# Second FFN of a two-block transformer layer: the modulation's place in the first steps, and its row products on TensorE

## The chip, the cores and the metric

One core of a Trainium2 chip runs the whole program. TensorE (PE) multiplies matrices into PSUM banks, VectorE (DVE), ScalarE (ACT) and GpSimd (POOL) work beside it, and SyncE (SP) and POOL issue the transfers that this text speaks of. The metric is the device time of one execution, in microseconds (us), as the median of several runs.

## The reference

Two transformer blocks follow each other on 512 tokens of width 1024. The first ends with a SwiGLU feed-forward network (here the second FFN of the program, called ffn2). The second block scales and shifts its norms by a modulation vector made from a conditioning vector c alone:

```python
x = x + 0.5 * swiglu(rms_norm(x, ffn2_norm[l]), ffn2_w_gate[l], ffn2_w_up[l], ffn2_w_down[l])
def swiglu(h, w_gate, w_up, w_down):
    return (jax.nn.silu(h @ w_gate) * (h @ w_up)) @ w_down
...
mod = (c_act @ w_mod[l] + b_mod[l])[:, None, :]      # c_act = silu(c), w_mod 1024 x 6144
sh1, sc1, g1, sh2, sc2, g2 = jnp.split(mod, N_MOD, axis=-1)
```

The second block also has an S5 state-space part, whose tables (powers and rotations of the state matrix, kernels inside chunks) depend on parameters alone.

## The kernel before

A weight matrix is read in panels of 1 MB (128 partitions x 2048 values). SP loads a panel into w_raw, ACT rounds it to its high part w_hi (L692), DVE subtracts to get the low part w_lo (L1188, split), and PE makes three products for each pair of tiles: high by high, low by high and high by low. There are two buffers of each kind: the gate panels use one, the up panels the other. SP loads the next panel into a buffer as soon as w_split says that its low part is made.

The gate and up products of ffn2 run over 11 steps. In a step PE makes 48 matmuls of the gate panel into banks 0 and 1 (by_k, L2004), then 48 of the up panel into banks 2 and 3. DVE scales the gate banks by the norm's root (L1391, "gate scaling"), ACT takes the SiLU, DVE multiplies by the up banks (L1401), and splits the product into high and low parts for the down product (L1236).

The first eight steps of ffn2 carry other work beside this, each in a loop of its own (PHASES). Steps 0 to 3 carry the last four of the modulation's twelve groups (ffn1's steps carry the first eight). For a group, DVE multiplies eight tiles of w_mod by one value of c_act per partition and adds them up (modulation, L1352 and L1355), splits the sum in two (L1360, L1362), and PE sums it over the partitions by two matmuls with a one-hot matrix (L2044, the row products), which put the group in a row of bank 6. POOL loads the tiles of w_mod, 256 KB each, into four slots (L568): the first four tiles of a group are there when it begins, and the load of tile 4 waits for DVE's use of tile 0, and so on, so that half of a group's tiles are loaded while it is computed. DVE may begin a group only when PE has made the row products of the group before it (semaphore mod_acc_free), since low part and sum lie in one place.

Behind each of the steps 0 to 3, DVE computes a part of the S5 tables (setup: s5_matrices, s5_first_angles, s5_second_angles, s5_powers). Steps 4 to 7 carry two pairs of chunk matrices each: DVE makes one pair ahead of the gate scaling and one behind the gate panel's low part (prepared, L1318 to L1329, 12 instructions each), and PE takes them behind the up products (chunk_pair, L2071 and L2080), first pair 0 and then pair 1. From step 4 on, prepared's first pair also waits until all twelve groups are in bank 6. All this is program order on each engine: an instruction that waits holds up whatever stands behind it.

Of the kernel before, what the change touches and what calls it, by code (L numbers as in the profile page):

```python
# [64 lines left out]
MOD_SLOTS = 4  # L65

MOD_STEPS = KD + 2
# [9 lines left out]
MOD_END = MOD_GROUPS - BESIDE_STEPS  # L77
# [3 lines left out]
MOD_STOP = {"ffn1": BESIDE_STEPS, "ffn2": MOD_END}  # L81
MOD_AT = {"ffn1": 0, "ffn2": BESIDE_STEPS}
# [50 lines left out]
def build(nc, inp, rel_onehot, out):  # L133
# [12 lines left out]
    with ExitStack() as ctx:  # L146
# [5 lines left out]
        def S(name):  # L152
            if name not in sems:
                sems[name] = ctx.enter_context(nc.semaphore(name))
            return sems[name]

        B = [ctx.enter_context(nc.psum_tensor(f"bank{i}", [P, T], F32)) for i in range(8)]
# [23 lines left out]
        row_of = sb("row_of", [P, 8], F32R)  # L181
# [183 lines left out]
        def paired(extra):  # L365

            return extra is not None and extra >= MOD_END
# [806 lines left out]
        def _(dve):  # L1174
            done = Steps(dve, S("dve_done"))

            def split(n, i=None):

                if i is None:
                    if n >= END:  # L1180
                        return
                    i = n
                dve.wait_ge(S("w_hi_done"), n + 1)
                if not isinstance(n, int) or n:

                    dve.wait_ge(S("w_split"), n)
                s = i % 2
                dve.tensor_tensor(w_lo[s][:], w_raw[s][:], w_hi[s][:].bitcast(F32), ALU.subtract).then_inc(S("w_split"), 1)  # L1188
# [175 lines left out]
            def swiglu(name):  # L1364
                base = BASE[name]
                setup = (s5_matrices, s5_first_angles, s5_second_angles, s5_powers)
                for start, stop, mods, extra in PHASES[name]:
                    if start == BESIDE_STEPS:

                        groups = sum(b - a for f in list(PHASES)[:list(PHASES).index(name) + 1] for a, b, m, _ in PHASES[f] if m)  # L1370
                        dve.wait_ge(S("mod_acc_free"), groups + 1)
                        dve.tensor_copy(tmp[0:8, 4, :], B[6][0:8, :]).then_inc(S("rows_made"), 1)
                        if name == "ffn2":
                            dve.wait_ge(S("pair_pe"), NS // 2)
                            for r in range(2):
                                dve.wait_ge(S(f"ca_stored{r}"), 32 * 4)
                                dve.wait_ge(S(f"pair_stored{r}"), 128 * 4)
                    with dve.Fori(start, stop) as i:
                        if start == 0:
                            modulation(i + MOD_AT[name], i, range(MOD_SLOTS))  # L1380
                            refined_root({"ffn1": "n1", "ffn2": "n2"}[name])
                            if name == "ffn1":
                                modulation(i + MOD_AT[name], i, range(MOD_SLOTS, KD))
                        elif mods:
                            modulation(i + MOD_AT[name], i)
                        if paired(extra):
                            prepared(extra, 0)
                        for t in range(2):
                            dve.wait_ge(S("pe_done"), i * 8 + (4 * base + 2 * t + 2))
                            dve.wait_ge(S("hid"), i * 2 + (HID[name] + t + 1))  # L1390
                            dve.tensor_tensor(tmp[:, t, :], B[t][:], rstd[:], ALU.mult).then_inc(S("gate_scaled"), 1)  # L1391
                        if start == 0 and name == "ffn2":
                            modulation(i + MOD_AT[name], i, range(MOD_SLOTS, KD))
                        split(i * 2 + (base + 2), base)
                        if paired(extra):
                            prepared(extra, 1)
                        for t in range(2):
                            dve.wait_ge(S("pe_done"), i * 8 + (4 * base + 4 + 2 * t + 2))
                            dve.wait_ge(S("silu"), i * 2 + (HID[name] + t + 3))
                            dve.wait_ge(S("hid_split"), i * 2 + (HID[name] + t + 1))  # L1400
                            dve.tensor_tensor(tmp[:, 2 + t, :], tmp[:, t, :], B[2 + t][:], ALU.mult).then_inc(S("hid"), 1)  # L1401
                        split(i * 2 + (base + 3), base + 1)
                        for t in range(2):
                            hid_lo_of(name, i, t, 2 + t)
                        if paired(extra):
                            kernels_read(extra)
                    if extra in range(MOD_END):
                        setup[extra]()

                first = 4 * MOD_AT[name]  # L1410
                last_col = 4 * groups
                dve.wait_ge(S("rows_t"), 2 * list(PHASES).index(name) + 5)
                turned = B[5][:, 0:32].rearrange("p (s g) -> p g s", s=4)[:, 0:groups - MOD_AT[name], :]
                dve.tensor_tensor(mod[:, first:last_col].rearrange("p (g s) -> p g s", s=4), turned,
                                  cols("b_mod_2")[:, first:last_col].rearrange("p (g s) -> p g s", s=4), ALU.add).then_inc(S("mod_made"), 1)
# [509 lines left out]
        def _(pe):  # L1925
# [83 lines left out]
            def first_gate(n, banks, h_name, between):  # L2009
# [10 lines left out]
                for k in range(KD):  # L2020
                    for t, bank in enumerate(banks):
                        mm = pe.matmul(bank[:], wl[:, k, t * P:(t + 1) * P], h_hi[:, k, :], start=False, stop=k == KD - 1)
                        if k == KD - 1:
                            mm.then_inc(S("pe_done"), 2)

            def gate_up(name, h_name, free, sums=None):

                base = BASE[name]
                for start, stop, mods, extra in PHASES.get(name, ((0, GU_STEPS, False, None),)):
                    with pe.Fori(start, stop) as i:  # L2030
                        for half in range(2):
                            if sums and start == 0 and half == 0:
                                first_gate(base, [B[0], B[1]], h_name, sums)
                                continue
                            pe.wait_ge(S("w_split"), i * 2 + (base + half + 1))
                            free(i, half)
                            wait = not sums and half == 0
                            by_k(base + half, [B[2 * half], B[2 * half + 1]], h_hi, h_lo, ready(h_name) if wait else None,
                                 wait_hi=ready_hi(h_name) if wait else None)
                        if mods:  # L2040

                            pe.wait_ge(S("mod_step"), i * MOD_STEPS + ((MOD_AT[name] + 1) * MOD_STEPS + MOD_SLOTS))
                            for part in (mod_hi, mod_lo):
                                mm = pe.matmul(B[6][0:8, :], row_of[:], part[:],  # L2044
                                               start=start == 0 and part is mod_hi, stop=stop == MOD_STOP[name] and part is mod_lo)
                            mm.then_inc(S("mod_acc_free"), 1)
                        if paired(extra):
                            for r in range(2):
                                chunk_pair(extra, r)
                    if name in PHASES and stop == GU_STEPS:  # L2050
                        pe.wait_ge(S("rows_made"), 2 * list(PHASES).index(name) + 2)
                        for s4 in range(4):
                            mm = pe.transpose(B[5][:, 8 * s4:8 * s4 + 8], tmp[0:8, 4, s4 * P:(s4 + 1) * P], ident[0:8, 0:8])
                        mm.then_inc(S("rows_t"), 1)
                    if name == "ffn2" and extra == 0:

                        pe.wait_ge(S("s5_landed"), 320)
                        for part in range(2):
                            for c in range(4):
                                mm = pe.transpose(B[4 + part][:, c * P:(c + 1) * P], c_in[:, part, c].rearrange("p w n -> p (w n)"), ident[:])  # L2060
                            mm.then_inc(S("c_t"), 1)
# [55 lines left out]
            for k in range(KD):  # L2117
# [3 lines left out]
                for b in range(TB):  # L2121
                    mm = pe.transpose(B[2 + k % 4][:, b * P:(b + 1) * P], x_in[:, b, k * P:(k + 1) * P], ident[:])
# [98 lines left out]
            for f in range(2):  # L2221
                for g in range(4):
                    mm = pe.transpose(B[6 + f][:, g * P:(g + 1) * P], ws_in[:, 4 * f + g, :], ident[:])
# [8 lines left out]
            for f in range(4):  # L2232
                for c in range(TB):
                    for half in range(2):
                        g = 2 * f + half
                        mm = pe.matmul(B[4 + f][64 * half:64 * half + 64, c * P:(c + 1) * P],
                                       vg[:, c, g * 64:(g + 1) * 64], wsT[:, g, :], start=True, stop=True)
# [406 lines left out]
```

## Time and profile before

| what | value |
|---|---|
| median of 3 runs | 1794.73 us (1794.62 to 1794.98) |
| profiled execution | 1793.39 us, span from first to last instruction 1791.9 us |
| PE busy | 1763.9 us, 98% of the span |
| DVE busy | 1069.7 us, 60% |
| ACT busy | 729.3 us, 41% |
| mean granted clock of PE | 0.999 of full speed |
| steps 1 to 4 of ffn2 | about 861 to 956 us from the span's start |

Lines in the views are those of the kernel before. The idle time in brackets stands ahead of an instruction on its engine, with what ended it. A busy PE is a pipeline with work in it, so stalls show as gaps between its rows.

### The profile page before, as it was taken

To read this page: it belongs to the slowest core of one execution; us is meant where nothing else is said; L and a number is where in the kernel's file an instruction comes from. 1 tells how busy PE (TensorE), PEld (TensorE's weight loads), DVE (VectorE), ACT (ScalarE), POOL (GpSimd) and SP (SyncE) were. 2 spreads that over 40 slices of the span, in tenths; PEclk is the share of its full clock that TensorE was granted. 3 is DMA by queue.
4 is the path that set the end of the run, shared out by engine and by line. 5 is a ranking of instruction groups with operands and counts; after the bars stand their busy time and mean duration, and the time that the engine had idled before them with its cause. 6 is when DMAs were issued, how large, how long until landed. Compare 5 with 4: busy or idle time off the path is not lost. (4 is left out here: it accounts for less than half of the span.)

```text
span 1791.9 us, 23429 instructions
## 1 busy us (share of the span) xinstructions
PE 1763.9 (98%) x8822; PEld 1437.1 (80%) x8822; DVE 1069.7 (60%) x1507; ACT 729.3 (41%) x1001; POOL 186.1 (10%) x239
## 2 busy tenths in 40 slices
PE   9999999999999999999999999999999999999998
PEld 6888888888887777788877888887986788888887
DVE  7666546655655676656888743436595655566433
ACT  4222222333435877423333222225465355555322
POOL 4222001210000000005211110210000300000000
PEclk9999999999999999999999999999999999999999
DMA  7777423343222121224554552325122222222232
GB/s 246 238 221 221 134 74 96 98 138 99 90 95 94 48 66 53 71 94 150 173 188 125 158 158 66 107 93 187 68 79 68 93 95 94 94 94 82 94 95 81
DMA packets 171694, 206.81 MB, mean 115 GB/s; under 512 B 18404, under 2 KB 150114, under 8 KB 171106
## 3 DMA queue, kind: packets, MB, share of 16 engines
q1 hardware_dynamic: 144994, 161.97, 27.9%
q0 software_dynamic: 12640, 38.55, 6.7%
q10 hardware_dynamic: 13984, 5.27, 1.1%
q8 instruction: 49, 0.80, 0.2%
q14 instruction: 27, 0.22, 0.0%
HBM read 190.29 MB, written 17.56 MB: 116 GB/s over the span
## 5 line engine op out<-in xcount | busy, mean ns | idle before, releaser
L692 ACT CAST w_hi<-w_raw 128x2048 fp32r<-128x2048 f32 x158 | 301.8, 1911 | 722.4 <-PE bank L2004 360.9
L1188 DVE TENSOR_TENSOR w_lo<-w_raw,w_hi 128x2048 fp32r<-128x2048 f32 x158 | 367.3, 2325 | 358.4 <-ACT w_hi L692 357.7
L2004 PE MATMUL bank<-h_hi,w_hi 128*128 128x512 f32 x1056 | 412.3, 390 | 3.5 <-DVE w_lo L1188 2.2
L2004 PE MATMUL bank<-h_hi,w_lo 128*128 128x512 f32 x1056 | 411.1, 389 | 0.0
L2004 PE MATMUL bank<-h_lo,w_hi 128*128 128x512 f32 x1056 | 325.4, 389 | 1.6 <-DVE h_lo L1231 1.6
L2004 PEld LDWEIGHTS bank<-h_hi,w_hi 128*128 128x128 f32 x1056 | 198.2, 188 | 49.5 <-issue 3.4
L2004 PEld LDWEIGHTS bank<-h_lo,w_hi 128*128 128x128 f32 x1056 | 198.2, 188 | 43.3 <-DVE h_lo L1231 2.0
L2004 PEld LDWEIGHTS bank<-h_hi,w_lo 128*128 128x128 f32 x1056 | 198.3, 188 | 41.0
L1961 PE MATMUL bank<-hid_hi,w_hi 128*128 128x512 f32 x528 | 205.6, 389 | 0.0
L1961 PE MATMUL bank<-hid_hi,w_lo 128*128 128x512 f32 x528 | 205.4, 389 | 0.0
L1961 PE MATMUL bank<-hid_lo,w_hi 128*128 128x512 f32 x528 | 205.4, 389 | 0.0
L611 POOL TENSOR_TENSOR tmp<-x 128x512 f32<-128x512 f32 x24 | 37.2, 1549 | 867.1 <-DVE x L1762 422.7
L1961 PEld LDWEIGHTS bank<-hid_hi,w_lo 128*128 128x128 f32 x528 | 99.1, 188 | 20.7
L1961 PEld LDWEIGHTS bank<-hid_hi,w_hi 128*128 128x128 f32 x528 | 99.1, 188 | 20.6
L1961 PEld LDWEIGHTS bank<-hid_lo,w_hi 128*128 128x128 f32 x528 | 99.1, 188 | 20.4
L1961 PE MATMUL bank<-w_hi,h_hi 128*128 128x512 f32 (+1 forms) x256 | 97.4, 380 | 0.7 <-DVE h_lo L1231 0.7
L1961 PE MATMUL bank<-w_hi,h_lo 128*128 128x512 f32 (+1 forms) x256 | 96.3, 376 | 0.0
L1961 PE MATMUL bank<-w_lo,h_hi 128*128 128x512 f32 (+1 forms) x256 | 96.2, 376 | 0.0
L1355 DVE SCALAR_TENSOR_TENSOR mod_acc<-mod_raw,small,mod_acc 128x512 f32<-128x512 f32 x84 | 63.1, 752 | 29.7 <-DMA mod_raw<-in_w_mod 25.6
L568 POOL DMA_DIRECT2D mod_raw<-in_w_mod x96 | 52.7, 550 | 174.5 <-DVE mod_acc L1352 123.1
L1401 DVE TENSOR_TENSOR tmp<-tmp,bank 128x512 f32<-128x512 f32 x44 | 28.3, 684 | 67.1 <-PE bank L2004 67.1
L1909 DVE SCALAR_TENSOR_TENSOR tmp<-bank,vec,tmp 128x511 f32<-128x511 f32 x88 | 63.8, 746 | 6.4 <-DVE tmp L1909 1.7
(442 smaller groups left out, 2464.8 us busy)
## 6 DMA issues: line engine op xcount, KB each, us to landing
w_raw<-in_w_in SPq DMA_DIRECT2D x29, 1024.0 KB, 5.0
mod_raw<-in_w_mod POOLq DMA_DIRECT2D x96, 256.0 KB, 4.1
w_raw<-in_ffn_w_gate SPq DMA_DIRECT2D x22, 1024.0 KB, 5.2
w_raw<-in_ffn_w_up SPq DMA_DIRECT2D x22, 1024.0 KB, 5.2
w_raw<-in_w_up SPq DMA_DIRECT2D x22, 1024.0 KB, 4.9
w_raw<-in_ffn_w_down SPq DMA_DIRECT2D x16, 768.0 KB, 4.6
w_raw<-in_ffn_w_down SPq DMA_DIRECT2D x16, 640.0 KB, 4.0
w_raw<-in_w_out SPq DMA_DIRECT2D x8, 1024.0 KB, 5.0
```

The source lines that it names most:

```text
L568: pool.dma_start(mod_raw[:, k % MOD_SLOTS, :], wm[:, k, bass.ds(i * T + first * T, T)])\
L611: done(pool.tensor_tensor(tmp[:, min(k, 1), :], x[:, k, :], x[:, k, :], ALU.mult))
L692: act.copy(w_hi[i % 2][:], w_raw[i % 2][:]).then_inc(S("w_hi_done"), 1)
L1188: dve.tensor_tensor(w_lo[s][:], w_raw[s][:], w_hi[s][:].bitcast(F32), ALU.subtract).then_inc(S("w_split"), 1)
L1355: ins = dve.scalar_tensor_tensor(mod_acc[:], mod_raw[:, k % MOD_SLOTS, :], small[:, k:k + 1], mod_acc[:], ALU.mult, ALU.add)
L1401: dve.tensor_tensor(tmp[:, 2 + t, :], tmp[:, t, :], B[2 + t][:], ALU.mult).then_inc(S("hid"), 1)
L1909: dve.scalar_tensor_tensor(y[:, back:], up[:, :T - back], col_at(f"conv_w_2:{2 - back}", i * 2, KF * half + t), y[:, back:], ALU.mult, ALU ...
L1961: mm = pe.matmul(out_ap, stationary, moving, start=first and i == 0, stop=last and i == total - 1)
L2004: mm = pe.matmul(bank[:], w[:, k, at], h[:, k, :], start=k == first and part == 0 and i == 0, stop=k == last and part == 1)
```

## The change

In the steps 1 to 3 of ffn2, DVE computes the modulation's group behind the gate scaling and the gate panel's low part, instead of ahead of both. On PE the row products of a group stand no longer behind the up products of its step: they stand between the gate and the up products of the next step (so group 0 of ffn2 in step 1, and group 3 in step 4, where no group is computed). ffn1 and ffn2's step 0 on DVE stay as they were.

```diff
--- before.py
+++ after.py
@@ -1381,7 +1381,7 @@
                             refined_root({"ffn1": "n1", "ffn2": "n2"}[name])
                             if name == "ffn1":
                                 modulation(i + MOD_AT[name], i, range(MOD_SLOTS, KD))
-                        elif mods:
+                        elif mods and name == "ffn1":
                             modulation(i + MOD_AT[name], i)
                         if paired(extra):
                             prepared(extra, 0)
@@ -1392,6 +1392,8 @@
                         if start == 0 and name == "ffn2":
                             modulation(i + MOD_AT[name], i, range(MOD_SLOTS, KD))
                         split(i * 2 + (base + 2), base)
+                        if mods and start and name == "ffn2":
+                            modulation(i + MOD_AT[name], i)
                         if paired(extra):
                             prepared(extra, 1)
                         for t in range(2):
@@ -2023,6 +2025,13 @@
                         if k == KD - 1:
                             mm.then_inc(S("pe_done"), 2)
 
+            def mod_rows(name, i, first, last, behind=0):
+
+                pe.wait_ge(S("mod_step"), i * MOD_STEPS + ((MOD_AT[name] + 1 - behind) * MOD_STEPS + MOD_SLOTS))
+                for part in (mod_hi, mod_lo):
+                    mm = pe.matmul(B[6][0:8, :], row_of[:], part[:], start=first and part is mod_hi, stop=last and part is mod_lo)
+                mm.then_inc(S("mod_acc_free"), 1)
+
             def gate_up(name, h_name, free, sums=None):
 
                 base = BASE[name]
@@ -2037,13 +2046,10 @@
                             wait = not sums and half == 0
                             by_k(base + half, [B[2 * half], B[2 * half + 1]], h_hi, h_lo, ready(h_name) if wait else None,
                                  wait_hi=ready_hi(h_name) if wait else None)
-                        if mods:
-
-                            pe.wait_ge(S("mod_step"), i * MOD_STEPS + ((MOD_AT[name] + 1) * MOD_STEPS + MOD_SLOTS))
-                            for part in (mod_hi, mod_lo):
-                                mm = pe.matmul(B[6][0:8, :], row_of[:], part[:],
-                                               start=start == 0 and part is mod_hi, stop=stop == MOD_STOP[name] and part is mod_lo)
-                            mm.then_inc(S("mod_acc_free"), 1)
+                            if name == "ffn2" and half == 0 and start in range(1, MOD_END + 1):
+                                mod_rows(name, i, start == 1, start == MOD_END, 1)
+                        if mods and name == "ffn1":
+                            mod_rows(name, i, start == 0, stop == MOD_STOP[name])
                         if paired(extra):
                             for r in range(2):
                                 chunk_pair(extra, r)
```

DVE, step 1 of ffn2, in program order: ahead of it are the last rows of s5_matrices, behind it s5_first_angles. Before:

```order
L1378 UNCONDITIONAL_BRANCH
L1348 CAST row_of<-one_hot 128x8
L1352 TENSOR_SCALAR mod_acc<-mod_raw,small 128x512
L1355 SCALAR_TENSOR_TENSOR mod_acc<-mod_raw,small,mod_acc 128x512 x7
L1360 CAST mod_hi<-mod_acc 128x512
L1362 TENSOR_TENSOR mod_lo<-mod_acc,mod_hi 128x512
L1391 TENSOR_TENSOR tmp<-bank,rstd 128x512 x2
L1188 TENSOR_TENSOR w_lo<-w_raw,w_hi 128x2048
L1401 TENSOR_TENSOR tmp<-tmp,bank 128x512 x2
L1188 TENSOR_TENSOR w_lo<-w_raw,w_hi 128x2048
```

After:

```order
L1378 UNCONDITIONAL_BRANCH
L1391 TENSOR_TENSOR tmp<-bank,rstd 128x512 x2
L1188 TENSOR_TENSOR w_lo<-w_raw,w_hi 128x2048
L1348 CAST row_of<-one_hot 128x8
L1352 TENSOR_SCALAR mod_acc<-mod_raw,small 128x512
L1355 SCALAR_TENSOR_TENSOR mod_acc<-mod_raw,small,mod_acc 128x512 x7
L1360 CAST mod_hi<-mod_acc 128x512
L1362 TENSOR_TENSOR mod_lo<-mod_acc,mod_hi 128x512
L1403 TENSOR_TENSOR tmp<-tmp,bank 128x512 x2
L1188 TENSOR_TENSOR w_lo<-w_raw,w_hi 128x2048
```

The gate scaling (bank, rstd) and the first w_lo now stand ahead of the seven mod_acc rows, and the product with the up banks (tmp, bank) behind mod_lo. The rows of steps 2 and 3 move in the same way.

PE, row products of ffn2 around step 1. Before, they end a step, and the branches of the loop follow (here the end of step 1):

```order
L2004 MATMUL bank<-h_hi,w_lo 128x512
L2004 MATMUL bank<-h_lo,w_hi 128x512 x2
L2044 MATMUL bank<-mod_hi,row_of 8x512
L2044 MATMUL bank<-mod_lo,row_of 8x512
L2030 REGISTER_ALU
L2030 COMPARE_AND_BRANCH
L2030 UNCONDITIONAL_BRANCH
L2004 MATMUL bank<-h_hi,w_hi 128x512
```

After, there are matmuls of the same step on both sides (here group 0 in step 1, between gate and up products):

```order
L2006 MATMUL bank<-h_hi,w_hi 128x512
L2006 MATMUL bank<-h_hi,w_lo 128x512
L2006 MATMUL bank<-h_lo,w_hi 128x512 x2
L2032 MATMUL bank<-mod_hi,row_of 8x512
L2032 MATMUL bank<-mod_lo,row_of 8x512
L2006 MATMUL bank<-h_hi,w_hi 128x512
L2006 MATMUL bank<-h_hi,w_lo 128x512
```

The two row products have moved by half a step, into the next step; their number is the same.

## Rows read from the trace of the kernel before

**Rows 1.** The page: the chain that ended last, by line.

```profile
PE bank L2004 23%; PE bank L1961 17%; PE bank L2366 1%; DVE w_lo L1188 1%; PE bank L1983 0%; DVE h_lo L1231 0%; DVE tmp L1221 0%; PE bank L2476 0%; PE bank L2080 0%; PE bank L2435 0%; PE bank L2405 0%; PE bank L2444 0%; ACT prob L1056 0%; PE bank L2501 0%; PE bank L2071 0%
```

**Rows 2.** The chain in order of time, 800 to 1050: start us, us, what.

```profile
931.70 1.09 DVE w_lo L1188
...
954.79 0.66 PE bank L2071 x4
...
956.42 22.03 PE bank L2004 x96
```

**Rows 3.** The timeline of PE: start us, us, instruction [idle before <-releaser].

```profile
905.41 0.40 PE L2044 MATMUL bank<-mod_lo,row_of 128*8 128x512 f32 x1
907.62 0.50 PE L2004 MATMUL bank<-h_hi,w_hi 128*128 128x512 f32 x1 [1.81 <-DVE w_lo L1188]
...
951.77 0.60 PE L2071 MATMUL bank<-ident,wb_in 128*128 128x128 f32 x4
...
954.79 0.66 PE L2071 MATMUL bank<-ident,wb_in 128*128 128x128 f32 x4 [1.44 <-DVE wb_in L1329]
```

**Rows 4.** The timeline of DVE, ffn2, steps 1 to 4.

```profile
870.09 0.17 DVE L1348 CAST row_of<-one_hot 128x8 fp32r<-128x8 f32 x1
...
880.35 2.28 DVE L1188 TENSOR_TENSOR w_lo<-w_raw,w_hi 128x2048 fp32r<-128x2048 f32 x1
...
888.54 0.30 DVE L1243 TENSOR_TENSOR tmp<-powers,s 128x144 f32<-128x144 f32 x1
...
904.09 1.28 DVE L1391 TENSOR_TENSOR tmp<-bank,rstd 128x512 f32<-128x512 f32 x2
905.29 2.28 DVE L1188 TENSOR_TENSOR w_lo<-w_raw,w_hi 128x2048 fp32r<-128x2048 f32 x1
...
912.09 0.68 DVE L1243 TENSOR_TENSOR angles<-powers,s 128x512 f32<-128x512 f32 x1
...
926.55 2.28 DVE L1188 TENSOR_TENSOR w_lo<-w_raw,w_hi 128x2048 fp32r<-128x2048 f32 x1
...
935.16 0.07 DVE L1283 MEMSET powers<- 128x16 f32 x1
...
954.31 0.42 DVE L1329 TENSOR_TENSOR wb_in<-tmp 128x256 f32<-128x256 f32 x1
```

**Rows 5.** The timeline of ACT, step 1: the next gate panel.

```profile
872.29 1.92 ACT L692 CAST w_hi<-w_raw 128x2048 fp32r<-128x2048 f32 x1 [9.29 <-PE bank L2004]
```

**Rows 6.** The timeline of SP, behind the w_lo of 880.35.

```profile
882.81 0.37 SPq L456 DMA_DIRECT2D w_raw<-in_ffn_w_gate  x1
```

**Rows 7.** mod_raw from 860 to 960 (three groups): waits in us, times; landing.

```profile
  DMA mod_raw<-in_w_mod: 4.3, 7
...
DMA to landing us min/median/max: 2.9/3.1/4.5
```

**Rows 8.** The same from 60 to 200, ffn1 (six groups).

```profile
  DMA mod_raw<-in_w_mod: 14.3, 12
...
DMA to landing us min/median/max: 3.2/4.2/6.2
```

**Rows 9.** The timeline of SP, in ffn1.

```profile
68.53 0.37 SPq L456 DMA_DIRECT2D w_raw<-in_ffn_w_up  x1
```

**Rows 10.** The timeline of DVE, ffn1: one group, and the gate scaling behind it.

```profile
69.63 0.17 DVE L1348 CAST row_of<-one_hot 128x8 fp32r x1
...
79.31 1.28 DVE L1391 TENSOR_TENSOR tmp<-bank,rstd 128x512 f32<-128x512 f32 x2
```

**Rows 11.** The timeline of PE behind an idle stretch of another stage.

```profile
1348.64 1.08 PE L2457 MATMUL bank<-pT,v 128*64 128x256 f32 x8 [2.88 <-ACT yat L1070]
...
1349.99 0.48 PE L1961 MATMUL bank<-z_lo,w_hi 128*128 128x512 f32 x1
...
1353.64 0.39 PE L1961 MATMUL bank<-z_lo,w_hi 128*128 128x512 f32 x1
```

**Rows 12.** Windows: us, PE, PEld, DVE, ACT, POOL busy (x), PEclk, DMA, GB/s.

```profile
1351.00:1352.00 1.00, 1.00 (x4) 0.71 (x4) 0.15 (x1) 1.00 (x3) 0.00 (x0) 0.50 0.00 0
```

## The prediction

> **What bounds the kernel now.** I read the page's chain first: TensorE's gate and up products (L2004, 23%) and down products (L1961, 17%) are its bulk, and all other lines are at 2% or below [rows 1]. So the kernel is a row of matmuls, and a change can move the end only by the few gaps in that row, and by what the other engines do to them. Then I read the chain in order of time around the changed steps. There it is not on PE throughout: it enters DVE at 931.70, in step 3, stays on DVE through the setup and the two pairs of step 4, and comes back to PE at 954.79; from 956.42 it is PE alone [rows 2]. The timeline of PE shows why. It has two gaps in steps 1 to 4: 1.81 us at 907.62, waiting for the low part of step 3's gate panel, and 1.44 us at 954.79, waiting for DVE's second pair of chunk matrices [rows 3]. Both are waits for DVE, and the second comes later. What reaches the end is therefore when DVE finishes its second pair in step 4 (954.31 plus 0.43 is 954.74 [rows 4]), whatever becomes of the first gap.
>
> **The change, part by part.** No instruction is added or taken away on any engine; only the order moves.
>
> The first gap. In step 2 DVE makes the group first, scales at 904.09 and makes the low part from 905.29, just too late for PE [rows 3, 4]. Behind the change this low part is made some 7 us earlier or better, so the gap of 1.81 us (with the restart 907.62 - 905.41 - 0.23 = 1.98) goes. PE then ends step 4's up products at 951.77 - 1.98 = 949.8. The row products' place costs nothing by itself: there are four groups ahead of that point before and after, and each pair takes 2 x 0.23 = 0.46 us (22.03/96 for one matmul of 512 columns [rows 2]). What is late next is the second pair: PE takes pair 0 in 1.6 us (954.79 to 956.42 for the other pair), is done at 951.4, and waits for DVE.
>
> DVE's own chain. It is the work of steps 1 to 4 plus DVE's idle time. Idle time that goes: from the gate panel's low part to the setup DVE takes 912.09 - 905.29 = 6.80 us in step 2, where it waits for nothing, but 888.54 - 880.35 = 8.19 in step 1 and 935.16 - 926.55 = 8.61 in step 3, where it waits for PE's up products and ACT's high part [rows 4]. With the group in between, PE and ACT are long ready there. That frees 1.39 + 1.81 = 3.2 us. Idle time that comes: in step 1 DVE is free at 870.1 [rows 4], but ACT's next gate panel starts at 872.29, when PE has left the buffer [rows 5]. It starts 0.46 earlier now, since group 0's row products are out of the way, so the low part can start at 871.83 + 1.92 = 873.8. The gate scaling fills 1.2 of the 3.7 us (905.29 - 904.09), so 2.5 us are idle. In steps 2 and 3 DVE runs behind PE and ACT and meets no new wait. The semaphore mod_acc_free, which now comes half a step later, is there in time: PE makes group 0's products at about 872.3, and DVE asks for them at 876.0. Step 4's first pair asks for group 3's at about 940 and later, and PE makes them at 938.5. The sum: 2.5 - 3.2 = -0.7 us, the second pair at 954.0.
>
> The transfers. SP issues the load of the next gate panel as soon as the low part is done: 0.2 us behind it [rows 6]. Before, the group was over by then. Now the 1 MB load starts together with the group, whose tiles 4 to 7 (another 1 MB) are loaded while it is computed and waited for at once. ffn1 shows what this costs: there the up panel's load is issued at 68.53 and the group starts at 69.63 [rows 9, 10]. Six such groups wait 14.3 us for their tiles, 2.38 each; ffn2's three, which meet no load, wait 4.3, 1.43 each [rows 7, 8]: 0.95 more. The median landing is 4.2 us against 3.1. By the whole length it is less: 79.31 - 69.63 = 9.68 us in ffn1 [rows 10], and 880.35 - 1.20 - 870.09 = 9.06 in ffn2 [rows 4]: 0.62 more. The changed order is no kinder than ffn1's: the panel's load has a start of about 1 us over the first tile load, not 2.3, so more of it overlaps. I take 0.8 per group, near the middle of the two readings; three groups make +2.4 us. The ends are 0 and, from the longest landing of 6.2 us against the median of 3.1, 3.1 per group; the rows of six groups lie near 0.6 to 1, so I keep 1.6 as a working upper end. The second pair is then ready at 954.0 + 2.4 = 956.4, that is 1.7 us later than before. POOL's queue holds nothing behind these loads, and the panel has from 876 to about 893 to land, so nobody else is late.
>
> The Trainium skill says the same of the mechanism ("DMA: Bandwidth & Descriptors", Issuing engines are not separate DMA queues): transfers started by SP and by POOL run on the same 16 engines and interleave. By this rule the low parts' early release speaks against the change; the landing times of ffn1 agree with it [rows 8].
>
> PE's clock. The gap in step 4 becomes 956.4 - 951.4 = 5.0 us, longer than any gap of the trace. Where PE had idled 2.88 us after a shorter gap, at 1348.64, its clock was granted at 0.50, the lower level of 1.2 GHz, a microsecond and a half later [rows 11, 12]: ten matmuls took 1353.64 - 1349.99 = 3.65 us instead of 2.3. That is 1.4 us, and the gap here is longer. Behind it stand step 5's matmuls, which are on the chain to the end. I take +1.4; the bounds are 0 (the clock stays) and 2.8 (twice such a stretch). The Trainium skill ("TensorE: Matmul & The Clock Gate", Part 1: The HAM clock gate) says that an idle array falls to half its clock and gets it back only by activity; here this rule makes the difference between the forecast and its nearest rival.
>
> Sum: -0.7 + 2.4 + 1.4 = +3.1 us. The profiled execution of 1793.39 (span 1791.9 and 1.5 around it) becomes 1796.5. The median of the runs is 1794.73, 1.3 above the profiled one, so 1797.8 is the forecast: slower by 0.17%.
>
> **The rivals.** First, the clock stays. For it: in the rows of the other stage two gaps stood close together, and here is one. Then the change costs -0.7 + 2.4 = +1.7, 1796.4.
>
> Second, the loads don't collide: the panel's and the tiles' packets pass each other without loss. Against it stand the 1.1 us between the landings of ffn1 and ffn2 [rows 7, 8]. Then the gap in step 4 is 954.0 - 951.4 = 2.6 us, the clock has less reason to fall, and the time is 1794.73 - 0.7 = 1794.0: the first gap goes and comes back in the second.
>
> Third, slower beyond what a measurement misses: the tile loads fall behind the panel's in earnest, since nearly the whole megabyte is ahead of them. It decides at the point where a group loses more than about 0.95 us, for then -0.7 + 3 x 0.95 + 1.4 passes 0.2% (3.6 us). At 1.6 per group the price is 4.8, and the sum -0.7 + 4.8 + 1.4 = +5.5: 1800.2. For it: the longest landing and the tighter overlap. Against it: six groups of ffn1 average under 1.
>
> Fourth, the change gives what the first gap holds: DVE would have to be early at the second pair too. DVE's chain there has no slack [rows 2], and all gaps of PE in these steps are 3.25 us [rows 3], so even both together stay under 0.2%. I allow it as 1794.73 - 2.0 = 1792.7.
>
> **How the numbers follow.** Forecast 0.45, clock stays 0.18, no collision 0.10, heavy collision 0.24, the gap given back 0.03. "Same" means within 0.2%, 3.6 us, about what a measurement of this kernel can tell from no change. Slower: the heavy collision, and a fifth of the forecast's own spread (0.62 to 0.95 per group, 1.0 to 1.8 for the clock, so +2.2 to +4.0): 0.24 + 0.09 = 0.33. Faster needs what no gap holds: 0.02. Same: 0.65. The range reaches from the second rival, 1794.0, to the third, 1800.2; it leaves out the fourth and the spread beyond 1.6 per group.
>
> **What would show it.** Right: no gap ahead of step 3's gate products; one of 4 to 6 us ahead of the second pair's transposes; the group's waits for mod_raw in 860 to 960 near 6.7 us in sum instead of 4.3; DVE idle about 2.5 us in step 1 and nothing ahead of its products with the up banks; a granted clock of about half behind the gap; step 5's first matmul at 958.1 at about half clock, where before it was 956.4. Wrong: a gap of 3 us or less in step 4 (no collision), a clock at 1.00 behind it, or any new gap of PE in steps 1 to 3, which would mean that the up panel's low part, now behind the group, comes too late for PE. By my times it is ready at about 889, 913 and 936 with the collisions, against PE's need at 894, 916 and 938: the margin is 2 us at the least, and a heavy collision would eat it.

## The result, and the profile after

The changed kernel takes 1799.19 us (median of 13 runs, 1797.88 to 1801.73); the kernel before, run beside it, 1794.69 (13 runs, 1791.55 to 1797.81). The ratio is 1.0026, 95% interval 1.0018 to 1.0033: 4.5 us slower, just past the 0.2% line, which the interval still touches. A second set of runs (5 of the changed kernel, 21 of the kernel before) gave 1799.13 against 1793.41, 1.0037 (1.0023 to 1.005), all of it past the line. The profiled execution took 1799.86 us with a span of 1798.3, 6.4 more than before's.

The page of the changed kernel, its first lines and the chain by engine:

```profile
span 1798.3 us, 23429 instructions
...
PE 1766.6 (98%) x8822; PEld 1438.3 (80%) x8822; DVE 1069.3 (59%) x1507; ACT 728.8 (41%) x1001; POOL 186.2 (10%) x239
...
PE 88%; DVE 6%; ACT 2%; issue 1%; DMA 1%; DVEq 0%; POOLq 0%; POOL 0%; ACTq 0%
```

DVE has as much to do as before (1069.7). The chain has a share of DMA, and DMA stands in it three times in the changed steps, as shown below. (The shares can't be set against those of the page of before, whose chain adds up to only 48% of the span.) The waits of PE from 800 to 1050 (total, times, longest) and those of DVE for the tiles from 860 to 960, answering to [rows 3, 7]:

```profile
PE bank L2077 <- DVE wb_in L1329: 7.9, 2, 6.9
PE bank L2006 <- DVE w_lo L1188: 0.3, 1, 0.3
```

```profile
  DMA mod_raw<-in_w_mod: 10.0, 4
...
DMA to landing us min/median/max: 3.0/4.5/5.6
```

The gap of 1.81 us ahead of step 3 is gone; the gap ahead of step 4's second pair grew from 1.44 us to 6.9. The tiles cost 10.0 us of waiting instead of 4.3. DVE's timeline shows where; its rows answer to [rows 4]:

```profile
871.30 1.29 DVE L1391 TENSOR_TENSOR tmp<-bank,rstd 128x512 f32<-128x512 f32 x2 [1.60 <-PE bank L2006]
873.52 2.29 DVE L1188 TENSOR_TENSOR w_lo<-w_raw,w_hi 128x2048 fp32r<-128x2048 f32 x1 [0.93 <-ACT w_hi L692]
875.73 0.17 DVE L1348 CAST row_of<-one_hot 128x8 fp32r<-128x8 f32 x1
...
882.15 3.32 DVE L1355 SCALAR_TENSOR_TENSOR mod_acc<-mod_raw,small,mod_acc 128x512 f32<-128x512 f32 x4 [3.29 <-DMA mod_raw<-in_w_mod]
...
886.68 1.28 DVE L1403 TENSOR_TENSOR tmp<-tmp,bank 128x512 f32<-128x512 f32 x2
...
907.54 0.75 DVE L1355 SCALAR_TENSOR_TENSOR mod_acc<-mod_raw,small,mod_acc 128x512 f32<-128x512 f32 x1 [3.17 <-DMA mod_raw<-in_w_mod]
908.89 2.47 DVE L1355 SCALAR_TENSOR_TENSOR mod_acc<-mod_raw,small,mod_acc 128x512 f32<-128x512 f32 x3 [0.60 <-DMA mod_raw<-in_w_mod]
...
931.07 3.31 DVE L1355 SCALAR_TENSOR_TENSOR mod_acc<-mod_raw,small,mod_acc 128x512 f32<-128x512 f32 x4 [2.94 <-DMA mod_raw<-in_w_mod]
```

Read it as three groups. Each runs through its first four tiles, which wait in their buffers, and then stands about 3 us for the fifth. A group, from row_of to the product behind it, takes 886.68 - 875.73 = 10.95 us in step 1, where it took 9.06. The traffic from 900 to 912, in step 2 (40 slices of 0.3 us), shows what the tiles land beside:

```profile
GB/s 0 0 0 0 0 0 0 0 48 85 177 215 317 372 386 386 386 389 389 423 413 410 396 423 369 369 423 382 137 27 27 27 14 0 0 0 0 0 0 0
```

From 904 to 908 the transfers move 370 to 420 GB/s without a break: the panel's megabyte and the four tiles' megabyte, all asked for between 901.5 and 905. The chain of work that ended last goes through these loads, in order of time (start, length, what):

```profile
876.92 5.20 DMA mod_raw<-in_w_mod
...
903.29 5.58 DMA mod_raw<-in_w_mod
...
926.19 4.86 DMA mod_raw<-in_w_mod
...
959.76 1.11 PE bank L2077 x4
960.88 1.82 PE bank L2086 x16
962.70 22.22 PE bank L2006 x96
```

So the path runs load, group, setup, pairs, and reaches PE at 959.76. PE's timeline there, and the windows (the column behind the busy counts is the granted clock):

```profile
951.27 0.66 PE L2077 MATMUL bank<-ident,wb_in 128*128 128x128 f32 x4 [1.08 <-DVE wb_in L1329]
951.85 1.05 PE L2086 MATMUL bank<-ca,bb 64*16 64x128 f32 x16
959.76 1.11 PE L2077 MATMUL bank<-ident,wb_in 128*128 128x128 f32 x4 [6.86 <-DVE wb_in L1329]
960.80 1.89 PE L2086 MATMUL bank<-ca,bb 64*16 64x128 f32 x16
```

```profile
954.00:956.00 2.00, 0.00 (x0) 0.00 (x0) 1.93 (x5) 0.87 (x1) 0.00 (x0) 1.00 0.09 9
956.00:958.00 2.00, 0.00 (x0) 0.00 (x0) 1.92 (x5) 0.00 (x0) 0.51 (x1) 0.57 0.94 264
958.00:960.00 2.00, 0.24 (x1) 0.24 (x2) 1.91 (x5) 0.00 (x0) 0.92 (x2) 0.50 1.03 376
960.00:962.00 2.00, 2.00 (x16) 1.38 (x17) 2.00 (x3) 1.66 (x3) 0.00 (x0) 0.50 0.03 10
962.00:964.00 2.00, 2.00 (x13) 1.35 (x9) 2.00 (x3) 0.04 (x1) 0.00 (x0) 0.72 0.13 33
964.00:966.00 2.00, 2.00 (x11) 1.62 (x10) 1.91 (x9) 0.00 (x0) 0.00 (x0) 1.00 0.65 188
```

The clock fell inside the gap and came back after 962, so the second pair's small products took 2.9 us instead of the first pair's 1.6. Step 5 begins at 962.63, 6.3 us later than before. Its first products still run at the lower clock: its 96 matmuls take 22.22 us, where they took 22.03 [rows 2]. Together that is 6.5 us, the difference of the two spans (6.4) to within 0.1.

### The profile page after: what moved, and what is told of

Its sections match the earlier page's. It is cut to its first block, busy times and chain, and to the rows that moved or that the text cites. A ratio compares the mean times of both kernels' runs of the same rounds, so it can differ in the third digit from the quotient of the medians.

```text
span 1798.3 us, 23429 instructions
## 1 busy us (share of the span) xinstructions
PE 1766.6 (98%) x8822; PEld 1438.3 (80%) x8822; DVE 1069.3 (59%) x1507; ACT 728.8 (41%) x1001; POOL 186.2 (10%) x239
## 4 chain that ended last, share of the span: by engine, by line
PE 88%; DVE 6%; ACT 2%; issue 1%; DMA 1%; DVEq 0%; POOLq 0%; POOL 0%; ACTq 0%
PE bank L2006 36%; PE bank L1963 36%; PE bank L2271 5%; DVE w_lo L1188 1%; PE bank L2372 1%; PE bank L2297 1%; PE bank L1931 1%; DMA mod_raw<-in_w_mod 1%; PE bank L1985 1%; PE bank L2165 1%; PE bank L2308 0%; DVE h_lo L1231 0%; DVE mod_acc L1355 0%; DVE tmp L1221 0%; PE bank L2086 0%
```

## The experiments

All kernels are the changed one with the edit shown; each ratio is to the kernel before, run on the same chip. The theory: DVE's chain to the second pair decides, the collision lengthens it (the panel's megabyte and the four tiles' megabyte are loaded at the same time, so the tiles land later), and the clock adds its part. Rivals are named with each run.

**late_load.** The panel's load waits until the group has used its last tile, in steps 1 to 3.

```diff
-                with sp.Fori(first, GU_STEPS) as i:
+                for start, stop in (((0, 3), (3, 4), (4, 5), (5, 6), (6, GU_STEPS)) if name == "ffn2" else ((first, GU_STEPS),)):
+                    with sp.Fori(start, stop) as i:
+                        if name == "ffn2" and start in (3, 4, 5):
+                            sp.wait_ge(S("mod_step"), (MOD_AT[name] + start - 2) * MOD_STEPS + MOD_SLOTS + 8)
```

> Theory (collision): the changed order lets SP load the next gate panel while the group's last four tiles are loaded, and DVE waits for them. Here the panel's load in steps 1 to 3 is held back until DVE has used the group's last tile; all else is the changed kernel. Expected: the group's waits for mod_raw in steps 1 to 3 fall from 10.0 us to about 4.3, the second pair is ready at 954.0 instead of 959.7, PE's gap ahead of it is 2.6 us, its clock stays at 1.00, and the time is 0.7 us below the kernel before (ratio 0.9996), 5 to 6 below the changed one. Rival (order): DVE's chain is longer because of the new order itself, by waits for PE or ACT; then the mod_raw waits may fall but the second pair stays near 959 and the time 4 to 6 us above before.

Measured: 1794.12 us, ratio 1.0000 (0.999 to 1.0009). The tiles' waits are back at before's, and PE's gap is short again, with the clock at 1.00:

```profile
  DMA mod_raw<-in_w_mod: 4.7, 7
```

```profile
954.93 0.66 PE L2080 MATMUL bank<-ident,wb_in 128*128 128x128 f32 x4 [2.96 <-DVE wb_in L1332]
955.52 1.05 PE L2089 MATMUL bank<-ca,bb 64*16 64x128 f32 x16
956.50 0.50 PE L2009 MATMUL bank<-h_hi,w_hi 128*128 128x512 f32 x1
```

The collision, with the clock's fall in the gap that it lengthens, is the whole loss. It isn't gone but moved to where nobody waits: in this run the panel goes out beside the next group's first tiles, and these land after up to 7.2 us, long before DVE asks for them. The run also shows the second rival's case as if by itself: without the collision the first gap goes and comes back in the second (2.96 us where I had worked out 2.6), and nothing is won.

**warm.** The changed order stays, and PE multiplies 28 times a constant into a free bank between the two pairs of step 4, so that it isn't idle in the gap. Ahead of them it waits until DVE has scaled the gate banks, since bank 0 is one of them.

```diff
                             for r in range(2):
                                 chunk_pair(extra, r)
+                                if extra == MOD_END and r == 0:
+                                    pe.wait_ge(S("gate_scaled"), HID[name] + 2 * MOD_END + 4)
+                                    for _ in range(28):
+                                        pe.matmul(B[0][:, 0:P], ones[:], ident[:], start=True, stop=True)
```

> The changed kernel with 28 idle products of 128 columns in bank 0 between pair 0 and pair 1 of step 4, so that PE is busy through most of its 6.9 us gap. Theory (clock): the granted clock stays at 1.00 through 950 to 966, pair 1's products take 1.6 us instead of 2.9 and step 5's first matmul runs at full rate, so that step 5 starts 1.2 us earlier behind the same DVE end, and the time is 1.5 us below the changed kernel (+3 to before). Rival: the clock plays no part, the pair's products are late for another reason, and the time is that of the changed kernel or above it.

Measured: 1797.26 us, ratio 1.0021 (1.0011 to 1.003).

```profile
951.18 6.52 PE L2059 MATMUL bank<-ident,ones 128*128 128x128 f32 x56
958.10 0.66 PE L2081 MATMUL bank<-ident,wb_in 128*128 128x128 f32 x4 [0.41 <-DVE wb_in L1329]
958.69 1.05 PE L2090 MATMUL bank<-ca,bb 64*16 64x128 f32 x16
959.67 0.50 PE L2006 MATMUL bank<-h_hi,w_hi 128*128 128x512 f32 x1
```

```profile
958.00:960.00 2.00, 1.90 (x21) 1.43 (x22) 2.00 (x4) 1.32 (x3) 0.00 (x0) 1.00 0.17 64
```

The clock stays at 1.00, and step 5 begins 959.67 - 958.10 = 1.6 us behind the pair's first transpose, not 962.63 - 959.76 = 2.9. That is 1.3 us. Step 5's 96 matmuls take 22.00 us here, so they give back another 0.2, and the clock's part in the changed kernel's first profile is 1.5 us. The medians lie 1.9 apart and the ratios 0.9 us, with intervals that overlap, so this figure rests on the traces.

**mid_load.** As late_load, but the panel's load is held only until the fourth tile is used (the same edit with `+ 4`).

> The changed kernel with the next gate panel's load held back, in steps 1 to 3, only until DVE has used the group's tile 3, so that the loads of tiles 4 to 6 are asked for first. If the transfers are served about in the order of their issue, the tiles pass first and the waits for mod_raw fall to 5 us or below, nearly as with the load held back to the end of the group. If they share in equal parts whatever the order, about 6 to 8 us stay. Time: 0 to 1 us above before by the first, 2 to 3 by the second.

Measured: 1803.42 us, ratio 1.0057 (1.0044 to 1.0071). Both expectations missed: it is worse than no hold at all (1.0037 in the same set of runs). DVE in step 1, and the DMA issues from 875 to 890 with their landing:

```profile
879.39 1.64 DVE L1358 SCALAR_TENSOR_TENSOR mod_acc<-mod_raw,small,mod_acc 128x512 f32<-128x512 f32 x2 [1.14 <-DMA mod_raw<-in_w_mod]
881.78 0.75 DVE L1358 SCALAR_TENSOR_TENSOR mod_acc<-mod_raw,small,mod_acc 128x512 f32<-128x512 f32 x1 [0.75 <-DMA mod_raw<-in_w_mod]
885.38 0.75 DVE L1358 SCALAR_TENSOR_TENSOR mod_acc<-mod_raw,small,mod_acc 128x512 f32<-128x512 f32 x1 [2.84 <-DMA mod_raw<-in_w_mod]
```

```profile
  DMA mod_raw<-in_w_mod: 14.7, 9
```

```profile
w_raw<-in_ffn_w_gate SPq DMA_DIRECT2D x1, 1024.0 KB, 7.9
```

The panel goes out when three of the tiles 4 to 7 have been asked for. In step 1, tiles 4 and 5 land in time as in late_load, tile 6 lands 0.75 us late, and tile 7, asked for 0.6 us behind the panel, lands only 6.5 us after it was asked for, when the traffic is nearly through. The low part of the up panel then comes too late for PE (4.0 us in two waits, the danger named in the prediction), and a gap of 6.6 us stands in step 4. So this later start of the load made the collision worse; no other point between it and the last tile was tried.

**rows_back.** DVE's order as changed, PE's row products back at the end of their own step.

```diff
-                            if name == "ffn2" and half == 0 and start in range(1, MOD_END + 1):
-                                mod_rows(name, i, start == 1, start == MOD_END, 1)
-                        if mods and name == "ffn1":
+                        if mods:
```

> The changed order on DVE alone: PE makes the row products at the end of the group's own step again and waits there for mod_lo. Theory (DVE's chain is what counts): PE now waits 3 to 4 us at the end of step 1 and up to 6 at the end of 2 and 3, but it would have waited for DVE in step 4 anyway; the second pair is ready within 1 us of the changed kernel's 959.7, the gaps are spread over four places, and the time is that of the changed kernel within 1.5 us, perhaps a microsecond less if the clock stays up. Rival (each gap of PE adds): the waits of 3 to 6 us per step come on top, +10 us and more.

Measured: 1807.88 us, ratio 1.0077 (1.0063 to 1.0091). I had expected the products' place to be nearly free. It is not; the rival in the expectation, that each gap of PE adds, came nearer. PE's three waits, of the kind that the change's PE part takes away, and the row of DVE in step 3:

```profile
886.75 0.60 PE L2032 MATMUL bank<-mod_hi,row_of 128*8 128x512 f32 x1 [4.19 <-DVE mod_lo L1362]
914.74 0.59 PE L2032 MATMUL bank<-mod_hi,row_of 128*8 128x512 f32 x1 [4.04 <-DVE mod_lo L1362]
942.61 0.59 PE L2032 MATMUL bank<-mod_hi,row_of 128*8 128x512 f32 x1 [4.23 <-DVE mod_lo L1362]
```

```profile
927.30 1.29 DVE L1391 TENSOR_TENSOR tmp<-bank,rstd 128x512 f32<-128x512 f32 x2 [3.59 <-PE bank L2006]
```

The sum is now made behind the low part, so PE stands for it at the end of each step; then its gate products come late, and DVE waits for them (3.59 us ahead of the scaling in step 3), and the wait goes round. With DVE's order as changed, the PE part is worth 8.7 us by the medians (1807.88 - 1799.19), which come from two sets of runs, and 9.1 by the two ratios.

**halves.** Tiles 0 to 3, which are there before the step begins, are computed where they were; only tiles 4 to 7 go behind the low part.

```diff
-                        elif mods and name == "ffn1":
-                            modulation(i + MOD_AT[name], i)
+                        elif mods:
+                            modulation(i + MOD_AT[name], i, range(KD if name == "ffn1" else MOD_SLOTS))
...
-                            modulation(i + MOD_AT[name], i)
+                            modulation(i + MOD_AT[name], i, range(MOD_SLOTS, KD))
```

> Steps 1 to 3 do the group's first four tiles ahead of the gate scaling (they have landed before) and the other four behind the low part. Theory (collision, and DVE's chain is what counts): tiles 4 to 7 are asked for before the panel's load starts and land while DVE scales and splits, so the waits for mod_raw fall to under 1 us in sum; the second pair is ready at about 952.5, PE waits there 1 to 1.5 us, and the time is 2 us below the kernel before (ratio 0.9989). Rival (order): it gains no more than the removed first gap gave in the changed kernel, and lies between before and after, +1 to +4 us.

Measured: 1791.02 us, ratio 0.9985 (0.9976 to 0.9994), faster than both kernels; against the kernel before it is clear of the noise, though less than 0.2%. No wait for tiles is left: the tiles' load runs while DVE scales the gate and makes the low part, and is through or nearly so when the panel's begins. The panels go out at 878.71, 901.49 and 923.13, which is 4.1 to 6.3 us earlier than before; the changed kernel's go out at 875.99, 901.50 and 925.26. Two of DVE's waits are new, for group 0's and 2's row products to free the accumulator, and one gap of PE stays:

```profile
871.89 0.17 DVE L1348 CAST row_of<-one_hot 128x8 fp32r<-128x8 f32 x1 [2.29 <-PE bank L2032]
...
916.41 0.17 DVE L1348 CAST row_of<-one_hot 128x8 fp32r<-128x8 f32 x1 [1.42 <-PE bank L2032]
```

```profile
952.42 0.66 PE L2077 MATMUL bank<-ident,wb_in 128*128 128x128 f32 x4 [1.46 <-DVE wb_in L1329]
```

**halves_end.** halves, with the row products back at the end of their step (the edit of rows_back), to take those waits away.

> The group in halves around the gate scaling, with PE's row products at the end of the group's own step as in the kernel before. Its sum is ready at about 883, when PE ends its up products. Theory: here PE's part of the change is not needed; DVE loses its waits of 2.3 and 1.4 us for the row products in steps 1 and 3 but waits for PE's up banks instead, and the time is that of the halves kernel within 1 us (ratio to before 0.998 to 0.999). Rival: a wait at a step's end comes on top at each group as it did with the group behind the low part, +2 us and more to the halves kernel.

Measured: 1792.37 us, ratio 0.9996 (0.9987 to 1.0005). PE waits 0.9 us once for mod_lo, the gap in step 4 is 1.42 us, and step 5 begins at 954.21, against 953.98 in halves. The traces are within 0.3 us of each other; the intervals overlap, so whether the products' place matters here stays open. DVE's two waits for row products are gone, but it waits 1.64 and 1.94 us for PE's up banks instead.

**filled.** halves, with 3.2 us of work that DVE does behind step 3 (the magnitudes and the table of skips) moved to behind step 0, to fill the first wait.

```diff
-            def s5_powers():
+            def s5_magnitudes():
...
+            def s5_powers():
+
                 dve.wait_ge(S("rot_made"), 2)
...
                         setup[extra]()
+                    if extra == 0:
+                        s5_magnitudes()
```

> The halves kernel, with 3.2 us of s5_powers (the magnitudes and the skip table, which wait for nothing) moved from behind step 3 to behind step 0, where DVE waits 2.3 us for PE. Theory (DVE's chain up to the second pair decides): the second pair is ready 1.5 to 3 us earlier, PE's gap of 1.46 us ahead of it goes, and the time is 1 to 1.5 us below the halves kernel, 3.5 to 4 us below before (ratio 0.998). Rival: step 1 becomes later by what was moved in, and it gives nothing.

Measured: 1791.13 us, ratio 0.9986 (0.9977 to 0.9995), no gain on halves. The first wait (2.29 us in halves) is filled, but another takes its place, in step 4:

```profile
938.61 0.46 DVE L1320 TENSOR_TENSOR tmp<-powers,cc 128x288 f32<-128x288 f32 x1 [3.43 <-PE bank L2036]
```

DVE's first pair waits for group 3's row products, which the change had moved half a step later. I had called this semaphore harmless; it is, as long as DVE is late itself.

**filled_last.** filled, with group 3's row products alone at the end of step 3.

```diff
-                            if name == "ffn2" and half == 0 and start in range(1, MOD_END + 1):
-                                mod_rows(name, i, start == 1, start == MOD_END, 1)
-                        if mods and name == "ffn1":
-                            mod_rows(name, i, start == 0, stop == MOD_STOP[name])
+                            if name == "ffn2" and half == 0 and start in range(1, MOD_END):
+                                mod_rows(name, i, start == 1, False, 1)
+                        if (mods and name == "ffn1") or (name == "ffn2" and start == MOD_END - 1):
+                            mod_rows(name, i, name == "ffn1" and start == 0, stop == MOD_STOP[name])
```

> The kernel filled with one edit: the row products of group 3 stand at the end of step 3 instead of behind the gate's products of step 4. In filled VectorE's first pair of step 4 waited 3.43 us, until 938.61, for those products to free the accumulator. Theory (that wait is what ends last in step 4 of filled): the first pair starts near 935, the second pair is ready near 949, TensorE's wait before the second pair's products (1.42 us at 952.32) is gone, and step 5 begins near 952.5; 1.4 us below filled, a ratio to the kernel before of 0.9978. The rival (VectorE does not reach the sum of group 3 earlier, since its own halves of work end only then, and TensorE waits 1 us or more for the low part of the sum at the end of step 3): a gain of less than 0.5 us on filled, a ratio of 0.9984 to 0.9992, and a wait of TensorE for mod_lo in the trace near 940.

Measured: 1789.79 us, ratio 0.9976 (0.9966 to 0.9986), the fastest of all. DVE ends its second pair early, and PE has no wait left from 860 to 975:

```profile
949.04 0.42 DVE L1331 TENSOR_TENSOR wb_in<-tmp 128x256 f32<-128x256 f32 x1
```

```profile
951.66 0.66 PE L2081 MATMUL bank<-ident,wb_in 128*128 128x128 f32 x4
952.25 1.05 PE L2090 MATMUL bank<-ca,bb 64*16 64x128 f32 x16
953.23 0.50 PE L2010 MATMUL bank<-h_hi,w_hi 128*128 128x512 f32 x1
```

The gap of 1.42 us is gone; step 5 begins at 953.23, 0.66 us earlier than in filled and 3.1 earlier than before. The start came 0.7 us later than I expected, because TensorE stands 0.8 us later at the up products' end than in filled. The medians come from two sets of runs; by their ratios (0.9976 and 0.9986) filled_last is 1.8 us ahead, with intervals that overlap, so that it is faster than filled isn't shown. Its profiled execution was the slowest of its nine (1791.94 us, a span of 1790.4 at a mean granted clock of 0.996, where filled has 1789.3 and 0.999): what step 5 gains, that execution loses outside the changed steps.

**after_again.** The changed kernel once more, beside mid_load, halves_end and filled.

> The changed kernel once more, for its spread from execution to execution. Theory (collision): the group's waits for mod_raw are again 8 to 11 us in sum, the second pair is 4 to 5 us later than before, PE's gap is 6 to 7 us with the clock at its lower level behind it, and the ratio to before is 1.002 to 1.003. Rival: the first profile was an outlier, and this one shows waits near 6 us and no drop of the clock.

Measured: ratio 1.0037, as given above. The tiles' waits from 860 to 960:

```profile
  DMA mod_raw<-in_w_mod: 8.3, 3
```

They cost 8.3 us, not 10.0, and step 5 begins at 961.49, 5.1 later than before; its 96 matmuls take 22.59 us, 0.6 more than before, the first of them at the lower clock. It is the same picture, with a collision and a share of the clock that vary from one execution to the next. Two more kernels load in the same order: the tiles cost 8.6 us in warm and 9.1 in rows_back.

## Why the prediction was right or wrong

The time was forecast at 1797.8 in a range of 1794.0 to 1800.2, and 1799.2 lies inside. The sign and the path were right. The likeliest class, within 0.2%, was not: +0.26% is slower, which had 0.33, though by its interval (0.18 to 0.33%) this set of runs alone doesn't settle it. That the time lies in the range is in part luck: the forecast for the profiled execution was +3.1 us, and it came out at +6.4. Step by step:

- The first gap goes and its place is taken by the second pair: right. No wait stands ahead of step 3, and the gap is one of waiting for DVE's second pair. The first pair came late too, by 1.08 us, which I hadn't worked out; it costs nothing, since PE has to wait for the second anyway. In after_again no such wait stands there.
- DVE's own chain, -0.7: right. Step 1 idles 1.60 + 0.93 = 2.53 us, where 2.5 was worked out. Nothing waits ahead of the products with the up banks. The second pair's products begin at 959.76, 5.0 later than before, and 5.0 is -0.7 plus the 5.7 us by which the tiles' waits grew. That it fits to a tenth is luck: the same difference gives -0.2 in after_again, -0.3 in late_load and -1.0 in warm, since the traces are already up to 0.7 us from before's at the start of step 1. With that taken off, the four give -0.3 to -0.9.
- The collision, +0.8 per group: the mechanism right, the size wrong. It measured (10.0 - 4.3)/3 = 1.9 us in the first profile and (8.3 - 4.3)/3 = 1.3 in the second; by the waits of warm and rows_back it is 1.4 and 1.6. All four lie above the 0.8, and the first above the 1.6 that was kept as the upper end. This is the step that failed: "I take 0.8 per group, near the middle of the two readings". Those readings came from ffn1, where the waits already hold a load beside the group, but one that starts further ahead. I noted that the overlap would be tighter, and then took the mean of the looser case. late_load, with 4.7 us of waits in all, shows that the load beside the group is the cause.
- A better estimate of the size, made only after the result: all that is asked for in one step is 2.1 MB, which at the traffic row's 390 to 420 GB/s takes some 5.2 us, against 3.1 for a tile without the panel: an estimate of 2.1 more per group. It fits the landing of 5.20 us in step 1, but no run confirms it as a rule: with the same bytes in flight, tiles took up to 7.1 us in mid_load. (The Trainium skill, "DMA: Bandwidth & Descriptors", Specifications, gives 435 GB/s as the fabric's ceiling for the 16 engines; by this figure the 2.1 MB would take 4.8 us, an estimate. The trace comes near the ceiling but doesn't test it: slices of 0.3 us reach 423 in step 2, while single slices of 0.4 us in step 1 read up to 453, above it, so one slice is a rough reading.)
- The clock, +1.4: the mechanism right, the size nearly so. The pair's small products cost 1.3 us more and step 5's matmuls 0.2 more, 1.5 in the first profile; in after_again it is 1.3 and 0.6, 1.9. The rows that the 1.4 came from were miscounted: between 1349.99 and 1353.64 nine matmuls start, not ten, so this stretch cost 3.65 - 9 x 0.23 = 1.6 us. The gap here was 6.9 us, where that stage had 2.88, and the prices are alike (1.5 and 1.9 against 1.6): in these traces the clock's price lay in the work behind the gap until the clock was back, not in the gap's length.
- The sum in the profile: -0.7 + 5.7 + 1.5 = +6.5, and the span is 6.4 longer. With the second profile's collision and clock it is -0.7 + 4.0 + 1.9 = +5.2, and its span is 5.6 longer. The medians say +4.5 and, in the second set, +5.7. So the forecast's three terms, with the collision at its measured size, account for the change to about half a microsecond. This is in substance the third rival (decided at 0.95 per group), which had 0.24.
- The margin of the up panel's low part, 2 us at the least by my times, was used up by the heavier collision: the one made in DVE's step 3 was ready near 939.0 instead of 936, and PE waited 0.3 us for it ahead of step 4's up products.
- mod_acc_free: right for this kernel. The runs halves and filled show that it is the next bound as soon as DVE is early.
- What I didn't weigh is that the row products' move is what makes DVE's new order bearable at all (rows_back, some 9 us more without it). I had priced their place at nothing, which holds only for the pair as a whole.

What stays open: why the collision is 1.9 us in one execution and 1.3 in another, why a panel that is asked for among the tiles holds the last of them longest (mid_load), and whether filled_last is faster than filled at all (0.66 us at step 5 in the traces, with interval bounds that would allow none).

## What to carry to other kernels

When an early release starts a big load, look at what small loads are being waited for at that moment. Don't size the delay as a mean over milder cases: all the bytes in flight over the rate that the traffic row shows came nearer here, as a first estimate. Work whose inputs are already there goes ahead of the release, and the work that still needs loads goes behind it (halves): this keeps both the early load and its cover. Once one wait is gone, ask which semaphore is next, for here two edits in a row (halves_end and filled) only put one wait in another's place, before the third took the last of them away.

## What the runs showed of the hardware

A 256 KB tile lands in 3.1 us (median of before) when no panel is loaded beside it. Where a 1 MB panel had been issued 1 to 4 us ahead on another queue, the tiles took 4.1 to 5.6 us, and the panel 5.2 to 5.5, near its median on the page of 5.3: the later loads paid. A panel issued behind three of four tiles (mid_load, step 1) landed after 7.9 us itself, and the tile behind it after 6.5, so there both paid. TensorE's clock went from 1.00 to 0.50 inside an idle stretch of 6.9 us, but stayed at 1.00 over 2.96 us (late_load); 28 small products (56 matmuls in the trace) in such a stretch kept it up at no cost that the trace shows. In the earlier stage of [rows 11] 2.88 us of idle time were followed by a lower clock, so the length of one gap alone doesn't tell whether the clock falls.
